# First tile ahead at the start of the second block's attention layers, and one weight chunk split by halves

## The chip, the cores and the metric

The kernel runs on one core of one Trainium2 chip. The metric is the device time of one execution in microseconds (us). PE is TensorE, DVE VectorE, ACT ScalarE, POOL GpSimd, SP the engine that issues most DMAs.

## The reference, cut to what matters

Two blocks of two transformer layers each, on 256 tokens of width 1024, all in float32. The second block is what the change touches, above all the two lines that begin a layer:

```
for l in range(2):
    proj = rms_norm(x, attn_norm[l]) @ w_in[l]        # [256, 1024] @ [1024, 2336]
    h_mla, h_diff, h_ch = split(proj, [416, 1568])
    o_mla  = rms_norm(mla_attention(h_mla, ...), mla_out_norm[l])
    o_diff = diff_attention(h_diff, ...)
    o_ch   = rms_norm(chunk_attention(h_ch, ...), chunk_out_norm[l])
    x = x + concat([o_mla, o_diff, o_ch]) @ w_out[l]
    x = x + conv_ffn(rms_norm(x, ffn_norm[l]), w_ffn_in[l], ..., w_ffn_out[l])
return rms_norm(x, final_norm)

def rms_norm(x, g):
    return x * rsqrt(mean(x * x, -1) + 1e-6) * g
```

## The kernel before

**Data and products.** The 256 tokens are two tiles of 128 rows, `X[:, t, :]` with `t` 0 or 1. Before a projection, the rows are scaled by the root of their mean square into `XH[:, t, :]`, transposed by PE in eight blocks of 128 features, and written as "features" `xh[:, k, tokens]` and `xl[:, k, tokens]`, `k` from 0 to 7. Each float32 factor is split in a high part (rounded, made by ACT: `xh`, `wh`) and a low part (the rest, made by DVE, for a few chunks by POOL: `xl`, `wl`), and one product is three matmuls, high x high, high x low, low x high (`mm3`). A matrix of weights comes in chunks of at most 1 MB: a DMA into one of four `raw` buffers, ACT's high part, DVE's low part, in two halves each. `J[name, i]` is a chunk's number, `weights(j)` splits a chunk on ACT and DVE, `weights_half(j, half)` half of it, `wait_chunk` makes PE wait for all of it. There are two places for split chunks, so that chunk n is split when PE has finished chunk n - 2 (`place_used`), and ACT and DVE run their own written order: each engine's program is a straight list of instructions, and they meet by semaphores.

**The start of a layer** (`l` 0 or 1; both look the same, with rows from a layer norm for l = 0, `own_rows`, and from an addition, `add_rows`, for l = 1). ACT squares each half row of both tiles (`square`), DVE adds the two sums (`mean_row`), POOL takes the power -1/2 (`rms`), DVE writes tile 0's scaled rows and the first half of tile 1's (`rms_rows`), ACT the second half of tile 1's (`rms_half`). PE first does `keep(0, 22)` or `keep(0, 6)`, matmuls of constants whose results are not used, then `rms_tiles`: for each k it transposes both tiles into one of four banks; ACT multiplies the 256 columns by the gain into `xh`, DVE makes `xl`. Then `part_tokens` multiplies chunks 0 and 1 of w_in (416 columns wide, four features each), for each feature both tiles:

```
            bs = {t: bank() for t in t2}
            part_tokens(0, 0, 416, bs, (win, 0))
            part_tokens(1, 1, 416, bs, (win, 0))
            for i in (2, 3, 4):
                for f in range(2):
                    column(i, f)
```

`column(i, f)` is 24 matmuls of 256 tokens by 128 columns of chunk i. Behind its features DVE has the distances between positions (`DIST`) and then chunk 2's low parts.

**The attention loop.** 11 units (six of two maps "diff", three "mla", two "chunk"). In turn i, PE does the transposes of unit i - 2, the scores of i, the values of i - 3, and some projection: in turn 4 and 5 `column(7, 0)` and `column(7, 1)` (chunk queries), in turn 6 and 7 chunk 8. DVE does in turn i `factors(i - 1)`, `turned`, the maxima of the scores of i, `normalise(i - 1)`, `mixed_low(i - 3)` (for odd diff units a reduction of squares that ACT makes after its exponentials of i), and then `beside(i)`, in which chunks are split: chunk 7 in turn 3, chunk 8 in turn 4, on ACT and DVE.

Of the kernel before, what the change touches and what calls it, by code (L numbers as in the profile page):

```python
# [144 lines left out]
def _build(nc, T, ctx):  # L145
# [3 lines left out]
    X = sb("X", [128, 4, 1024])  # L149
# [308 lines left out]
    def tensor_program(e, q):  # L458
# [486 lines left out]
        for l in range(2):  # L945
            A = ATT2[l]
            key, win = A.key, f"win{l}"
            span[:] = [0, 6]
            keep(0, (22, 6)[l])
            rms_tiles(("a", l), ("x1", 1) if l == 0 else ("f", 0))  # L950
            nb[0] = 5
            side = (S.ea, S.ev)
            side = (S.ea, S.ev)

            def part_tokens(i, part, w, bs, key):

                j = J[win, i]
                hv, lv = (v.rearrange("p (k n) -> p k n", k=4) for v in (hi_of(j), lo_of(j)))
                wait_chunk(j)
                for t in t2 if part == 0 else ():  # L960
                    wait_bank(bs[t])
                for k in range(4):
                    x = 4 * part + k
                    wait_feature(("a", l), x)
                    for t in t2:
                        tk = slice(128 * t, 128 * t + 128)
                        m = mm3(ps[bs[t]][:, 0:w], (xh[:, x, tk], xl[:, x, tk]), (hv[:, k, :], lv[:, k, :]), x == 0, x == 7)
                        if k == 3:
                            m.then_inc(*S.proj.up((key, t), ("use", j)))
                for t in t2 if part == 1 else ():  # L970
                    BANK[key, t] = bs[t]
                    free[bs[t]] = [(side[t], (key, t))]

            def column(i, f):

                j, b = J[win, i], bank()
                hv, lv = (v.rearrange("p (k n) -> p k n", k=8) for v in (hi_of(j), lo_of(j)))
                fs = slice(128 * f, 128 * f + 128)
                wait_chunk(j)
                wait_bank(b)  # L980
                for k in range(8):
                    m = mm3(ps[b][:, 0:256], (hv[:, k, fs], lv[:, k, fs]), (xh[:, k, 0:256], xl[:, k, 0:256]), k == 0, k == 7)
                m.then_inc(*S.proj.up(((win, i), f), ("use", j)))
                BANK[(win, i), f] = b
                free[b] = [(side[f], ((win, i), f))]
# [186 lines left out]

            bs = {t: bank() for t in t2}
            part_tokens(0, 0, 416, bs, (win, 0))
            part_tokens(1, 1, 416, bs, (win, 0))
            for i in (2, 3, 4):
# [111 lines left out]

    def feature_cols(key):
        g = key[2] if key[0] == "f" else key[1] if key[0] == "f1" else 0  # L1290
        return slice(256 * g, 256 * g + 256)

    def feature_slot(k):
# [7 lines left out]
    def feature_scales(key, k):  # L1301

        if key[0] in ("f", "f1"):
            g = key[-1]
            return sc[:, 0, k, g:g + 1], sc[:, 1, k, g:g + 1]
        kind, l = key
# [6 lines left out]
    def scalar_program(e, q):  # L1313
# [25 lines left out]
        def features(key, ks=range(8), wait=()):  # L1339

            for k in ks:
                q.wait_ge(*S.tr.at((key, k)))
                src, dst = ps[BANK.get((key, k), 0)][:, 0:256], xh[:, k, feature_cols(key)]
                s, s2 = feature_scales(key, k)
# [277 lines left out]
        block1_ffn(1, 1)  # L1622
        for t in t2:
            for half in range(2):
                square(("x1", 1), t, half, (S.vec, ("row", t, half)))
        rms_half(("x1", 1))


        for l in range(2):
# [12 lines left out]

            features(("a", l), wait=[(S.proj, ("use", used))])
            weights(after(J[win, 0]))
# [59 lines left out]
            def beside(i):  # L1704
# [8 lines left out]
                elif i == 10:  # L1713
                    turned_high(i)
                if i in (1, 2, 3, 4, 6, 8, 10):
                    weights(after({1: J[win, 5], 2: J[win, 6], 3: J[f"uq{l}", 0], 4: J[f"ukv{l}", 0], 6: J[win, 7],
                                   8: J[win, 8], 10: J[win, 9]}[i]))
# [29 lines left out]
            for t in t2:  # L1747
                for half in range(2):
                    square(("f", l), t, half, (S.vec, ("taken", f"fout{l}", t, half)))
            if l == 0:  # L1750
                rms_half(("f", l))

    def vector_program(e, q):
# [48 lines left out]
        def low(key, k):  # L1804
# [3 lines left out]
            if feature_kind(key) == "each":  # L1808
                r = e.scalar_tensor_tensor(dst, ps[BANK.get((key, k), 0)][:, 0:256], feature_scales(key, k)[0], high,
                                           ALU.mult, ALU.subtract)  # L1810
            else:
                r = e.tensor_tensor(dst, feature_slot(k), high, ALU.subtract)
# [490 lines left out]
        def own_rows(t, sides=(0, 1)):  # L2303
# [22 lines left out]
        own_rows(1, (1,))  # L2326
        rms_rows(("x1", 1), 0)
        mean_row(("x1", 1), 1)
        rms_rows(("x1", 1), 1, 512)


        for l in range(2):
# [17 lines left out]

            features(("a", l))
            for t, ks in enumerate(A.tiles):
# [141 lines left out]
            def beside(i):  # L2494
# [70 lines left out]
            if l == 0:  # L2565
                rms_rows(("f", l), 0)
                mean_row(("f", l), 1)
                rms_rows(("f", l), 1, 512)

# [15 lines left out]
    def gpsimd_program(e, q):  # L2585
# [145 lines left out]
    def sync_program(e, q):  # L2731
# [5 lines left out]
        for j, (name, i, w, kind) in enumerate(ORDER):  # L2737
# [24 lines left out]
            elif (name, i) in (("win0", 3), ("win1", 3)):  # L2762
                l = int(name[3])
                q.wait_ge(*S.tr.at((("a", l), 7)))
                e.dma_start(CB[:, :, :], T["rel"][l]).then_inc(*S.rel.up(l, by=16))
# [145 lines left out]
```

## Time and profile before

| | us |
|---|---|
| time, median of 3 runs | 1646.96 |
| lowest, highest | 1645.0, 1647.8 |
| the profiled execution, its time | 1644.66 |
| the profiled execution, span from first to last instruction | 1643.0 |
| PE busy in the span | 1597.2 (97%) |
| DVE, ACT, POOL busy | 1048.6 (64%), 804.0 (49%), 235.4 (14%) |

PE's busy time counts a matmul from its start to its modelled end, and matmuls overlap; keep matmuls count as busy too. Lines of the kernel in the profile (L486) are those of the program printed above; a helper's line serves all its callers: L486 to L488 are the three matmuls of `mm3`, L479 is `keep`, L528 the transposes of features, L1348 and L1809 their high and low parts, L1330 and L1775 the high and low parts of weights, L1443 `square`, L1449 `rms_half`, L2018 `rms_rows`, L2596 POOL's power.

### The profile page before, as it was taken

How to read it: one execution, taken by the hardware profiler on the slowest of the kernel's cores; microseconds unless marked ns; L12 is line 12 of the kernel's file. 1: busy time of each engine (PE TensorE's matmuls, PEld its weight loads, DVE VectorE, ACT ScalarE, POOL GpSimd, SP SyncE). 2: the span in 40 equal slices, each digit the busy share in tenths (PEclk: the TensorE clock that was granted, in tenths of full speed). 3: DMA queues.
4: the chain of work that ended last, by engine and by line, in shares of the span. 5: the costliest groups of instructions: out<-in, count | busy, mean ns of one | idle time of the engine just before them, and what ended most of it. 6: DMA issues, size and time to landing. Idle time of an engine off the chain costs nothing.

```text
span 1643.0 us, 26992 instructions
## 1 busy us (share of the span) xinstructions
PE 1597.2 (97%) x10894; PEld 1379.3 (84%) x10894; DVE 1048.6 (64%) x1938; ACT 804.0 (49%) x1517; POOL 235.4 (14%) x282
## 2 busy tenths in 40 slices
PE   7999999999999999999999999999999999999998
PEld 4788778887777888887899988878999888789986
DVE  3735856465354425787787767766776667767765
ACT  2414963332233423567455553655555556555553
POOL 0202410010110000012011101132111013311110
PEclk9999999999999999999999999999999999999999
DMA  9765122454564234021455552424555533335552
GB/s 368 291 243 200 37 81 84 157 202 154 214 253 174 77 103 154 10 76 45 180 180 206 180 195 106 149 83 154 180 180 184 191 136 125 129 135 189 186 197 77
DMA packets 39851, 257.28 MB, mean 157 GB/s; under 512 B 5552, under 2 KB 6832, under 8 KB 11056
## 3 DMA queue, kind: packets, MB, share of 16 engines
q1 hardware_dynamic: 36848, 249.61, 41.9%
q0 software_dynamic: 1296, 4.72, 0.9%
q8 instruction: 87, 1.43, 0.3%
q10 hardware_dynamic: 1584, 1.23, 0.2%
q14 instruction: 36, 0.29, 0.1%
HBM read 254.49 MB, written 1.05 MB: 156 GB/s over the span
## 4 chain that ended last, share of the span: by engine, by line
PE 83%; DVE 9%; ACT 4%; issue 2%; DMA 1%; ACTq 0%; POOL 0%; DVEq 0%; SPq 0%
PE ps L486 25%; PE ps L488 24%; PE ps L487 24%; PE ps L502 3%; PE ps L633 1%; PE ps L655 1%; PE ps L642 1%; DVE ps L2034 1%; DVE wl L1775 1%; PE ps L528 1%; PE ps L1081 1%; ACT arena L1681 1%; ACT wh L1330 1%; PE ps L614 1%; ACT arena L1401 1%
## 5 line engine op out<-in xcount | busy, mean ns | idle before, releaser
L1775 DVE TENSOR_TENSOR wl<-raw,wh 128x1024 fp32r<-128x1024 f32 (+2 forms) x322 | 375.9, 1209 | 349.8 <-ACT wh L1330 349.2
L1330 ACT CAST wh<-raw 128x1024 fp32r<-128x1024 f32 (+1 forms) x332 | 326.7, 1034 | 490.0 <-PE ps L488 400.3
L486 PE MATMUL ps<-xh,wh 128*128 128x256 f32 (+1 forms) x1582 | 493.5, 312 | 2.7 <-issue 2.4
L488 PE MATMUL ps<-xh,wl 128*128 128x256 f32 (+1 forms) x1582 | 488.6, 309 | 0.0
L487 PE MATMUL ps<-xl,wh 128*128 128x256 f32 (+1 forms) x1582 | 488.5, 309 | 0.0
L486 PEld LDWEIGHTS ps<-xh,wh 128*128 128x128 f32 x1582 | 301.8, 191 | 28.0 <-issue 12.0
L488 PEld LDWEIGHTS ps<-xh,wl 128*128 128x128 f32 x1582 | 301.8, 191 | 15.3
L487 PEld LDWEIGHTS ps<-xl,wh 128*128 128x128 f32 x1582 | 301.9, 191 | 15.1 <-issue 0.7
L486 PE MATMUL ps<-wh,xh 128*128 128x512 f32 (+3 forms) x812 | 297.7, 367 | 1.0 <-issue 0.8
L488 PE MATMUL ps<-wh,xl 128*128 128x512 f32 (+3 forms) x812 | 293.2, 361 | 0.0
L487 PE MATMUL ps<-wl,xh 128*128 128x512 f32 (+3 forms) x812 | 293.1, 361 | 0.0
L2119 DVE SCALAR_TENSOR_TENSOR arena<-ps,pv,arena 128x254 f32<-128x254 f32 (+2 forms) x352 | 192.6, 547 | 16.2 <-ACT arena L1495 6.9
L486 PEld LDWEIGHTS ps<-wh,xh 128*128 128x128 f32 x812 | 153.1, 189 | 30.0 <-issue 7.5
L488 PEld LDWEIGHTS ps<-wh,xl 128*128 128x128 f32 x812 | 153.1, 189 | 22.7
L487 PEld LDWEIGHTS ps<-wl,xh 128*128 128x128 f32 x812 | 153.3, 189 | 21.8 <-issue 0.5
L2636 POOL TENSOR_TENSOR arena<-arena 128x256 f32<-128x256 f32 (+1 forms) x88 | 81.9, 931 | 608.1 <-ACT arena L1480 608.1
L2596 POOL TENSOR_TENSOR st<-st,cs 128x1 f32<-128x1 f32 (+2 forms) x46 | 37.6, 818 | 510.4 <-DVE st L1951 236.3
L1495 ACT ACTIVATE arena<-ps,pv 128x256 f32<-128x256 f32 (+1 forms) x176 | 98.8, 609 | 13.7 <-PE ps L488 13.7
L502 PE MATMUL ps<-raw,silp 128*32 128x256 f32 x768 | 49.6, 393 | 9.2 <-DVE silp L2143 7.5
L1401 ACT ACTIVATE arena<-ps,st 128x512 f32<-128x512 f32 (+1 forms) x80 | 49.9, 644 | 8.8 <-DVE st L2034 5.0
L2626 POOL TENSOR_SCALAR arena<-arena,st 128x512 f32<-128x512 f32 (+1 forms) x40 | 34.4, 865 | 137.5 <-DVE st L2064 137.5
L1681 ACT ACTIVATE arena<-ps,st 128x128 f32<-128x128 f32 x88 | 35.9, 420 | 37.1 <-DVE st L2410 19.3
(214 smaller groups left out, 1835.8 us busy)
## 6 DMA issues: line engine op xcount, KB each, us to landing
raw<-in_ada SPq DMA_DIRECT2D x48, 1024.0 KB, 6.2
raw<-in_up SPq DMA_DIRECT2D x44, 1024.0 KB, 5.0
raw<-in_fin SPq DMA_DIRECT2D x44, 1024.0 KB, 4.8
raw<-in_down SPq DMA_DIRECT2D x22, 1024.0 KB, 4.8
raw<-in_fout SPq DMA_DIRECT2D x22, 1024.0 KB, 4.8
raw<-in_win SPq DMA_DIRECT2D x12, 1024.0 KB, 4.9
raw<-in_ev_w_in SPq DMA_DIRECT2D x9, 1024.0 KB, 7.1
raw<-in_wout SPq DMA_DIRECT2D x8, 1024.0 KB, 4.9
```

The lines of the kernel that those rows point to most:

```text
L486: e.matmul(out, A[0], B[0], start=first, stop=False)
L487: e.matmul(out, A[0], B[1], start=False, stop=False)
L488: return e.matmul(out, A[1], B[0], start=False, stop=last)
L502: m = e.matmul(ps[b][32 * g:32 * g + 32, 0:256], silp[:, k, 14 - 2 * i:46 - 2 * i], wv[:, k, :], start=(i == 0 and k < 4), stop=(last and ...
L1330: e.copy(hi_of(j)[:, a:b], raw_of(j)[:, a:b]).then_inc(*S.hi.up((j, half)))
L1401: e.activation(A.P[A.slot(i)][:, m, ks], A.scores(i)[:, m, ks], ACT.Exp, bias=mx[:, n:n + 1], scale=-1.0 if key == "od" or u["h"] >= 8 els ...
L1495: e.activation(temp(up, f)[:, part, 0:n], ps[2 * (f % 3) + part][:, 0:n], ACT.Identity, bias=w[3], scale=w[1 if up[0] == "u" else 2]).then ...
L1681: e.activation(A.P(i)[:, m, ks], ps[m][:, ks], ACT.Exp, bias=mx[:, c:c + 1], scale=1.0 if A.kind(i) == "mla" else -1.0, accum_out=sm[:, c: ...
L1775: e.tensor_tensor(lo_of(j)[:, a:b], raw_of(j)[:, a:b], hi_of(j)[:, a:b].bitcast(F), ALU.subtract).then_inc(*S.lo.up((j, half)))
L2119: e.scalar_tensor_tensor(acc[:, :, lo:hi], src[:, :, lo + shift:hi + shift], conv(row, f + NT * part), acc[:, :, lo:hi], ALU.mult, ALU.add ...
L2596: e.tensor_tensor(out, in_, minus_half[:, 0:n], ALU.pow).then_inc(*S.gps.up(key))
L2636: e.tensor_tensor(ACTF[:, f, 0:n], t[:, 1, 0:n], t[:, 0, 0:n], ALU.mult).then_inc(*S.prod.up((up, f)))
```

## The change

On all engines the first tile's features and products are put ahead of the second tile's. Features now have keys `("a", l, t)` and are 128 columns wide. ACT scales tile 0's rows (`rms_first`), DVE the first half of tile 1's, ACT its second half. PE's keep is 16 and 3 instead of 22 and 6. PE's products of chunks 0 and 1 are `first_rows(t, xs, bs)`, three matmuls for each tile and feature. `column` waits for its chunk by halves. The splits of chunk 7 move: on ACT half 0 ahead of turn 3's exponentials and half 1 behind them; on DVE half 0 in turn 3 and half 1 in turn 4; chunk 8's low parts on DVE from turn 4 to turn 5.

```
-            keep(0, (22, 6)[l])
-            rms_tiles(("a", l), ("x1", 1) if l == 0 else ("f", 0))
+            keep(0, (16, 3)[l])
...
+            made = ("x1", 1) if l == 0 else ("f", 0)
+            def first_features(t, ks):
+                features(("a", l, t), (t,), ks, [6, 7, 2, 3, 4, 5] if t else [4, 5, 6, 7, 2, 3],
+                         lambda k: [(S.act if t == 0 or k >= 4 else S.vec, ("xr", *made, t, k // 4))])
+            def first_rows(t, xs, bs):
+                tk = slice(128 * t, 128 * t + 128)
+                for x in xs:
+                    j = J[win, x // 4]
+                    hv, lv = (v.rearrange("p (k n) -> p k n", k=4) for v in (hi_of(j), lo_of(j)))
+                    if x % 4 == 0:
+                        wait_chunk(j)
+                    if x == 0:
+                        wait_bank(bs[t])
+                    wait_feature(("a", l, t), x)
+                    m = mm3(ps[bs[t]][:, 0:416], (xh[:, x, tk], xl[:, x, tk]), (hv[:, x % 4, :], lv[:, x % 4, :]), x == 0, x == 7)
...
# column(i, f), PE
-                wait_chunk(j)
                 wait_bank(b)
                 for k in range(8):
+                    q.wait_ge(*S.hi.at((j, k // 4)))
+                    q.wait_ge(*low_done(j, k // 4))
...
             bs = {t: bank() for t in t2}
-            part_tokens(0, 0, 416, bs, (win, 0))
-            part_tokens(1, 1, 416, bs, (win, 0))
+            first_features(0, range(6))
+            first_rows(0, [0], bs)
+            first_features(0, [6])
+            first_rows(0, [1], bs)
+            first_features(0, [7])
+            first_rows(0, [2, 3, 4], bs)
+            for x in range(5, 8):
+                first_features(1, [2 * x - 10, 2 * x - 9])
+                first_rows(0, [x], bs)
+            for x in range(2):
+                first_rows(1, [x], bs)
+                first_features(1, [6 + x])
+            first_rows(1, range(2, 8), bs)
...
# ACT
+        def rms_first(key):
+            q.wait_ge(*S.gps.at(("rs", key, 0)))
+            for half in range(2):
+                hs = slice(512 * half, 512 * half + 512)
+                e.mul(XH[:, 0, hs], X[:, 0, hs], cols((key, 0, "r"), 1)).then_inc(*S.act.up(("xr", *key, 0, half)))
+        def first_tile(l, key, last, used):
+            wait = [(S.proj, ("use", used))]
+            features(("a", l, 0), [0], wait)
+            square(key, 1, 1, last)
+            features(("a", l, 0), range(1, 4), wait)
+            rms_half(key)
+            features(("a", l, 0), range(4, 8), wait)
...
# ACT, ahead of layer 0 (ahead of layer 1 the same with ("f", 0))
-        for t in t2:
-            for half in range(2):
-                square(("x1", 1), t, half, (S.vec, ("row", t, half)))
-        rms_half(("x1", 1))
+        for half in range(2):
+            square(("x1", 1), 0, half, (S.vec, ("row", 0, half)))
+        rms_first(("x1", 1))
+        square(("x1", 1), 1, 0, (S.vec, ("row", 1, 0)))
...
-            features(("a", l), wait=[(S.proj, ("use", used))])
+            first_tile(l, ("x1", 1) if l == 0 else ("f", 0),
+                       (S.vec, ("row", 1, 1) if l == 0 else ("taken", "fout0", 1, 1)), used)
+            features(("a", l, 1))
             weights(after(J[win, 0]))
...
# ACT, the loop; beside(3) had weights(chunk 7)
+                if i == 3:
+                    weights_half(J[win, 7], 1)
...
             for i in range(A.n + A.lag + 1):
                 if 0 <= i - A.lag < A.n:
                     turned(i - A.lag)
+                if i == 3:
+                    weights_half(J[win, 7], 0)
                 if i < A.n:
                     softmax(i)
...
# DVE
+        def first_tile(l, key):
+            low(("a", l, 0), 0)
+            mean_row(key, 1)
+            low(("a", l, 0), 1)
+            low(("a", l, 0), 2)
+            rms_rows(key, 1, 512)
+            for k in range(3, 8):
+                low(("a", l, 0), k)
...
-        rms_rows(("x1", 1), 0)
-        mean_row(("x1", 1), 1)
-        rms_rows(("x1", 1), 1, 512)
+        first_tile(0, ("x1", 1))
...
-            features(("a", l))
+            features(("a", l, 1))
...
# DVE, beside(i)
                 elif i == 3:
                     copy2(("kn", l, 1), KN[:, 1, :])
+                    weights_half(J[win, 7], 0)
                 elif i == 4:
+                    weights_half(J[win, 7], 1)
                     copy2(("vm", l, 1), VM[:, 1, :])
...
-                if i in (1, 2, 3, 4, 11):
-                    weights(after({1: J[win, 5], 2: J[win, 6], 3: J[f"uq{l}", 0], 4: J[f"ukv{l}", 0], 11: J[win, 9]}[i]))
+                if i in (1, 2, 5, 11):
+                    weights(after({1: J[win, 5], 2: J[win, 6], 5: J[f"ukv{l}", 0], 11: J[win, 9]}[i]))
...
# POOL (rotation product) and SP (table of chunk attention, ahead of chunks 4 and later)
-            q.wait_ge(*S.tr.at((("a", l), 7)))
+            q.wait_ge(*S.tr.at((("a", l, 1), 7)))
```

## Rows read from the trace of the kernel before

**Rows 1.** The page's chain that ended last, by engine, share of the span
```profile
PE 83%; DVE 9%; ACT 4%; issue 2%; DMA 1%; ACTq 0%; POOL 0%; DVEq 0%; SPq 0%
```
**Rows 2.** Timeline of PE, start of layer 0: start, length, what, idle before
```profile
989.29 9.66 PE L479 MATMUL ps<-cs 128*128 128x256 f32 x44
1000.77 1.06 PE L528 MATMUL ps<-cs,arena 128*128 128x128 f32 x8 [1.83 <-DVE arena L2018]
1002.36 1.94 PE L528 MATMUL ps<-cs,arena 128*128 128x128 f32 x8 [0.52 <-DVE xl L1809]
1003.95 0.70 PE L486 MATMUL ps<-home,xh 128*128 128x416 f32 x1
...
1005.14 0.47 PE L486 MATMUL ps<-home,xh 128*128 128x416 f32 x1
...
1013.72 0.28 PE L486 MATMUL ps<-xh,wh 128*128 128x256 f32 x1
```
**Rows 3.** Timeline of PE, start of layer 1, and transposes before its feed-forward part
```profile
1316.58 2.75 PE L479 MATMUL ps<-cs 128*128 128x256 f32 x12
1319.78 1.06 PE L528 MATMUL ps<-cs,arena 128*128 128x128 f32 x8 [0.45 <-DVE arena L2018]
...
1322.67 0.42 PE L486 MATMUL ps<-home,xh 128*128 128x416 f32 x1
...
1331.79 0.28 PE L486 MATMUL ps<-xh,wh 128*128 128x256 f32 x1
...
1446.70 1.06 PE L528 MATMUL ps<-cs,arena 128*128 128x128 f32 x8 [2.14 <-DVE arena L2018]
```
**Rows 4.** Windows of 1 us: busy time by engine, granted PE clock third from last
```profile
1002.00:1003.00 1.00, 0.64 (x3) 0.63 (x4) 1.00 (x4) 0.79 (x3) 0.00 (x0) 0.50 0.00 0
...
1005.00:1006.00 1.00, 1.00 (x5) 0.97 (x5) 0.97 (x4) 1.00 (x2) 0.08 (x1) 0.81 0.26 49
...
1446.00:1447.00 1.00, 0.30 (x3) 0.33 (x4) 0.49 (x1) 0.72 (x1) 0.03 (x1) 1.00 0.12 49
```
**Rows 5.** Timelines of POOL, ACT and DVE, start of layer 0; last, a narrow ACT operation
```profile
994.89 1.06 POOL L2596 TENSOR_TENSOR st<-st,cs 128x1 f32<-128x1 f32 x2 [6.68 <-DVE st L1951]
998.49 0.63 ACT L1443 ACTIVATE arena<-X 128x512 f32<-128x512 f32 x1 [0.73 <-DVE X L2315]
...
1000.14 0.72 ACT L1449 ACTIVATE arena<-X,st 128x512 f32<-128x512 f32 x1 [0.93 <-POOL st L2596]
1001.22 1.57 ACT L1348 ACTIVATE xh<-ps,pv 128x256 fp32r<-128x256 f32 x4 [0.36 <-PE ps L528]
...
1000.14 0.48 DVE L2018 TENSOR_SCALAR arena<-X,st 128x512 f32<-128x512 f32 x1 [0.66 <-POOL st L2596]
1001.73 1.66 DVE L1809 SCALAR_TENSOR_TENSOR xl<-ps,pv,xh 128x256 fp32r<-128x256 f32 x4 [1.10 <-ACT xh L1348]
...
1036.01 0.37 ACT L1681 ACTIVATE arena<-ps,st 128x128 f32<-128x128 f32 x1 [0.51 <-DVE st L2410]
```
**Rows 6.** Timelines of POOL and ACT, start of layer 1
```profile
1314.89 0.54 POOL L2596 TENSOR_TENSOR st<-st,cs 128x1 f32<-128x1 f32 x1 [51.19 <-DVE st L2012]
...
1317.50 0.63 ACT L1443 ACTIVATE arena<-X 128x512 f32<-128x512 f32 x1 [2.00 <-DVE X L2559]
```
**Rows 7.** Timeline of DVE, low parts of chunks 2 and 3, layer 0
```profile
1006.56 2.28 DVE L1775 TENSOR_TENSOR wl<-raw,wh 128x1024 fp32r<-128x1024 f32 x2
...
1016.37 3.21 DVE L1775 TENSOR_TENSOR wl<-raw,wh 128x1024 fp32r<-128x1024 f32 x2 [0.39 <-ACT wh L1330]
```
**Rows 8.** Timelines of ACT, DVE and PE around chunk 7, layer 0
```profile
1052.04 0.37 ACT L1681 ACTIVATE arena<-ps,st 128x128 f32<-128x128 f32 x1 [1.53 <-DVE st L2410]
...
1055.27 2.36 DVE L1775 TENSOR_TENSOR wl<-raw,wh 128x1024 fp32r<-128x1024 f32 x2 [1.63 <-ACT wh L1330]
...
1057.73 0.36 PE L486 MATMUL ps<-xh,wh 128*128 128x256 f32 x1 [1.05 <-issue]
...
1066.64 0.55 PE L1092 MATMUL ps<-cs,arena 128*128 128x128 f32 x3 [0.89 <-DVE arena L2433]
```

More of the change, by code:

```diff
@@ L948, in tensor_program @@
             span[:] = [0, 6]
-            keep(0, (22, 6)[l])
-            rms_tiles(("a", l), ("x1", 1) if l == 0 else ("f", 0))
+            keep(0, (16, 3)[l])
             nb[0] = 5
             side = (S.ea, S.ev)
-            side = (S.ea, S.ev)
+            made = ("x1", 1) if l == 0 else ("f", 0)
[13 more added lines that the diff above has]
+                    m = mm3(ps[bs[t]][:, 0:416], (xh[:, x, tk], xl[:, x, tk]), (hv[:, x % 4, :], lv[:, x % 4, :]), x == 0, x == 7)
+                    if x == 7:
+                        m.then_inc(*S.proj.up(((win, 0), t), *([("use", j)] if t else [])))
+                    elif x == 3 and t:
+                        m.then_inc(*S.proj.up(("use", j)))
+                BANK[(win, 0), t] = bs[t]
+                free[bs[t]] = [(side[t], ((win, 0), t))]
             def part_tokens(i, part, w, bs, key):
@@ L963, in part_tokens @@
                     x = 4 * part + k
-                    wait_feature(("a", l), x)
                     for t in t2:
@@ L1289, in feature_cols, with feature_width @@
     def feature_cols(key):
+        if key[0] == "a":
+            return slice(128 * key[2], 128 * key[2] + 128)
         g = key[2] if key[0] == "f" else key[1] if key[0] == "f1" else 0
         return slice(256 * g, 256 * g + 256)
+    def feature_width(key):
+        return 128 if key[0] == "a" else 256
     def feature_slot(k):
@@ L1305, in feature_scales @@
             return sc[:, 0, k, g:g + 1], sc[:, 1, k, g:g + 1]
-        kind, l = key
+        kind, l = key[:2]
         if kind == "m":
@@ L1342, in features @@
                 q.wait_ge(*S.tr.at((key, k)))
-                src, dst = ps[BANK.get((key, k), 0)][:, 0:256], xh[:, k, feature_cols(key)]
+                src, dst = ps[BANK.get((key, k), 0)][:, 0:feature_width(key)], xh[:, k, feature_cols(key)]
                 s, s2 = feature_scales(key, k)
@@ L1714, in beside @@
                     turned_high(i)
-                if i in (1, 2, 3, 4, 6, 8, 10):
-                    weights(after({1: J[win, 5], 2: J[win, 6], 3: J[f"uq{l}", 0], 4: J[f"ukv{l}", 0], 6: J[win, 7],
+                if i == 3:
+                    weights_half(J[win, 7], 1)
+                if i in (1, 2, 4, 6, 8, 10):
+                    weights(after({1: J[win, 5], 2: J[win, 6], 4: J[f"ukv{l}", 0], 6: J[win, 7],
                                    8: J[win, 8], 10: J[win, 9]}[i]))
@@ L1748, in scalar_program @@
                 for half in range(2):
-                    square(("f", l), t, half, (S.vec, ("taken", f"fout{l}", t, half)))
+                    if l or not t or not half:
+                        square(("f", l), t, half, (S.vec, ("taken", f"fout{l}", t, half)))
             if l == 0:
-                rms_half(("f", l))
+                rms_first(("f", l))
     def vector_program(e, q):
@@ L1808, in low @@
             if feature_kind(key) == "each":
-                r = e.scalar_tensor_tensor(dst, ps[BANK.get((key, k), 0)][:, 0:256], feature_scales(key, k)[0], high,
+                r = e.scalar_tensor_tensor(dst, ps[BANK.get((key, k), 0)][:, 0:feature_width(key)], feature_scales(key, k)[0], high,
                                            ALU.mult, ALU.subtract)
@@ L2565, in vector_program @@
             if l == 0:
-                rms_rows(("f", l), 0)
-                mean_row(("f", l), 1)
-                rms_rows(("f", l), 1, 512)
+                first_tile(1, ("f", l))
         def final_rows(t, half):
@@ L2763, in sync_program @@
                 l = int(name[3])
-                q.wait_ge(*S.tr.at((("a", l), 7)))
+                q.wait_ge(*S.tr.at((("a", l, 1), 7)))
                 e.dma_start(CB[:, :, :], T["rel"][l]).then_inc(*S.rel.up(l, by=16))
```

## The prediction

> **What bounds the kernel now.** I read the page first, then the PE timeline at the two places that the change names, then what ACT, DVE and POOL do just ahead of them. The chain that ended last is PE for 83% [rows 1], so a microsecond counts only where PE stands still or does nothing useful. The start of each layer of the second block is such a place. In layer 0 the last product of the block before is issued by 989.29; then come 22 keep-warm matmuls (44 records, 9.66 us), an idle 1.83 us, eight transposes, an idle 0.52 us, eight more, and the first product at 1003.95. The first 416 columns take 16 product rows (8 features by 2 tiles) of three matmuls; they end where the next product starts, 1013.72 [rows 2]. In layer 1 the same: 1316.58, six keep matmuls, first transposes 1319.78, first product 1322.67, next stage 1331.79 [rows 3]. So a start costs 14.7 us in layer 0 and 6.1 us in layer 1, in which PE does no product. What holds the products back is in the ACT, DVE and POOL rows: the squares of the second tile's last half (ACT 998.49), its root on POOL, for which ACT stands idle 0.93 us, the scaled rows (1000.14, 0.72 us), then feature by feature ACT's high part and DVE's low part of both tiles together [rows 5]. The first tile was ready long before: its root is the second of the two POOL operations from 994.89, that is 995.95 [rows 5]. The kernel makes its first product wait for the second tile.
>
> **Part 1: the first tile by itself, layer 0.** Nothing is added to PE: 16 transposes and 48 matmuls remain, in another order; keep falls from 22 to 16 matmuls, at 9.66/22 = 0.44 us each, so it ends at 989.29 + 7.03 = 996.3. ACT takes the first tile's scaling from DVE: two halves of 512 at 0.72 us (about 0.64 apart): 995.98 to 997.3. Then the square of (tile 1, half 0) until 998.0, and the first feature. A feature is now 128 columns wide. Nothing in this stage shows that width; the nearest is an ACT operation of 128x128 from PSUM that lasts 0.37 us alone; the 256-wide ones come 1.57/4 = 0.39 (ACT) and 1.66/4 = 0.42 us (DVE) apart [rows 5]. I take 0.28 and 0.26 us per feature, a fixed part and a part that halves (bounds: half of the wide ones, 0.20, and all of it, 0.42). So 16 narrow features cost ACT 4.5 instead of 3.2 us, DVE 4.2 instead of 3.4.
> The path from there: high part of feature 0 done 998.35, low part 998.7, first product 998.85 (an estimate of 0.15 from DVE to PE: the idle 0.52 between the transposes less one feature's 0.39 [rows 2, 5]). ACT then turns to the square of (1,1) at 998.49 as before, so features 1 to 3 come at 999.2 to 1000.1, their low parts from 999.6; DVE's half of the second tile's rows lies between (1000.14 to 1000.6), ACT's too (until 1000.8). Product row 1 (three matmuls at (1013.72 - 1003.95)/48 = 0.20, 0.19 in layer 1, so 0.57) starts at 1000.05, and from there low parts arrive every 0.3 to 0.6 us, with feature 4's at about 1001.5: PE is the slower of the two. Left are 15 rows of 0.57 = 8.55 us and ten transposes of about 0.13 (1.06/8) = 1.3 us. The stage ends at 1000.05 + 9.85 = 1009.9 instead of 1013.72: 3.8 us gained, if PE runs at 2.4 GHz.
>
> **The clock.** In layer 0 the granted clock is 0.50 (1.2 GHz) at 1002 to 1003, after PE had stood idle 1.83 and 0.52 us with eight transposes between. At 1446.70 PE had stood idle 2.14 us and then did the same eight transposes [rows 3], and the clock stayed at 1.00 [rows 4]. So such a stretch may cost the clock or not. The loss now is the two starts' difference from first transposes to next stage: 12.95 against 12.01 us [rows 2, 3], 0.9 us. After the change PE is as thinly fed from 996.3 to 1000 (idle about 2.3 us of 3.7); if the clock falls, rows 1 to 4 run at the rate of the slow rows (three matmuls from 1003.95 to 1005.14, 0.40 us each at most against 0.19 [rows 2]; I take 0.35), costing about 1.5 us. Layer 0 is thus worth 3.8 (clock lost now, kept after), 2.9 (kept in both) or 2.3 (lost in both). Executions will differ; I take 2.9 for the median.
> The Trainium skill, "TensorE: Matmul & The Clock Gate", Part 4: PE-mode transpose, says that transposes do not count as PE being busy for the clock. By that rule the layer-0 fall is as it should be, but the stretch at 1446.70 speaks against it; it would bring the fall in layer 1 too, which is rival 1: by the rule the sum is 3.3 us, by the row 5.4.
>
> **Layer 1.** The first tile is ready while PE still multiplies: its root starts at 1314.89 [rows 6], ACT's two halves end at 1316.8. Keep is 3 matmuls, ending 1317.95. Feature 0's high part 1318.4 to 1318.8, first product 1319.25. ACT meets feature 0 before the square of (1,1), which slips from 1317.50 [rows 6] to 1318.7, and all behind it nearly by as much; row 1 of the products starts at 1320.3, and 9.85 us on is 1330.1 against 1331.79: 1.7 us. The keep matmuls cost 0.7 of it: with none the first product could start earlier.
>
> **What comes behind the start.** The second tile's transposes are spread between products, so its last features leave ACT at about 1006.9 instead of 1004.71, and only then does ACT split the next weights (win chunk 2), DVE after it: half 0's low part at about 1009.7, half 1's at 1010.9, where before both were done at 1008.84 (1006.56 + 2.28) [rows 7]. PE wants them at 1009.9 and, since a column now waits by half, 1011.4: nothing lost, 0.3 at most. Chunk 3: DVE ended it at 1019.58, just as PE needed it (1013.72 + 5.8), slowed by POOL to 3.21 us for what else takes 2.28 [rows 7]. After: ACT 1012.2 to 1014.2, DVE until 1016.3; PE needs half 0 at 1015.7 and half 1 at 1017.2. Covered with 0.9 to spare, and without the half-wait it would cost 0.6. The SP queue's table load stands behind the last transpose, 1004.30 before (1002.36 + 1.94 [rows 2]), at about 1006.3 now, with three chunks queued behind; the next is wanted at 1015.7, so this is hidden by 4 us. POOL's rotation product too.
>
> **Part 2: chunk 7 by halves.** PE waits 1.05 us at 1057.73 for chunk 7, whose low parts DVE makes 1055.27 to 1057.63 after waiting 1.63 for ACT, while ACT had stood idle 1.53 before the exponentials at 1052.04 [rows 8]. Half 0 on ACT moves into that idle time (free). DVE then does half 0 at 1053.6 to 1054.8 and goes on to the next unit's maxima, 2.7 us earlier than before. But half 1 stands on DVE behind a reduction that waits for ACT's square, which ACT makes after the four exponentials (1.6 us from their start); these start at 1055.9 now, so I get 1058.0 for the reduction and 1059.7 for half 1. So PE starts column 7 at once (1056.7), stops in its middle 1.6 us, and is 0.7 us late at the next unit. There it gets that back and more: the 0.89 us wait at 1066.64 for DVE [rows 8] is gone, because chunk 8's split, which stood before that unit's maxima, now stands behind them. Net 0.35 to 0.45 us a layer, 0.8 for both. Bounds per layer: -0.7 (nothing comes back) to +1.9 (both waits gone).
>
> **Sum.** 2.9 + 1.7 + 0.8 = 5.4 us. The profiled execution (1644.66, span 1643.0) lost the clock in layer 0; against it the sum is 3.8 + 1.7 + 0.8 = 6.3, or 1638.4. The median of the runs is 2.3 us above it, and nothing in the trace says that this difference goes: 1646.96 - 5.4 = 1641.5.
>
> **Rivals.**
> 1. Clock lost in both layers: layer 0 2.3, layer 1 1.7 - 1.5 = 0.2, with 0.8: 3.3 us, 1643.7. For it: in layer 1 PE has a thin stretch from 1317.95 to 1320.3. Against: it holds some 0.9 us of idle time only, less than the 2.14 that cost nothing. 0.10. By the rule named above, of the Trainium skill, this is the case that comes; by the row at 1446.70 it is not.
> 2. The gain is given back at chunk 3 (or 2): DVE now does 16 low parts and is itself late; if narrow features cost as much as wide ones (0.42), DVE is 2.6 us later in each start, PE is fed at 0.42 instead of 0.57 per row, still enough, but chunk 2 comes at 1012.3, whose second half PE wanted at 1011.4, and chunk 3 near 1018, wanted at 1017.2; with POOL's slowing (3.21 - 2.28 = 0.9) on top about 2 us are gone in each layer: 5.4 - 3.9 = 1.5 us, 1645.5. 0.12.
> 3. Slower: the clock, once down, stays at 1.2 GHz through the products, since these are now fed one row at a time. A matmul then costs 0.35 instead of 0.19. It decides from (5.4 + 3.3)/0.16 = 54 slow matmuls of the 96 in both layers; all 96 would cost 15 us: 1646.96 - 5.4 + 15 = 1656.6. Against: the clock is back within 1005 to 1006 after four matmuls in a row [rows 2, 4]. Chance of slower 0.06.
> 4. The change does not do what it says: if the first tile's products wait for something else of the second tile. The only such order is ACT's square (1,1) between features 0 and 1 (counted). 0.05 for 0 to 1 us: 1646.5.
> 5. More: both chunk-7 waits go and the clock holds: 3.8 + 1.7 + 2 x 1.5 = 8.5, 1638.5. 0.07.
>
> **Numbers.** Forecast 0.60. Its own range is 2.3 + 1.4 + 0 to 3.8 + 2.0 + 2 = 3.7 to 7.8 us: 1639.2 to 1643.3. The asked range adds rival 5 and most of 1 and 2: 1638.6 to 1645.3. 0.2% is 3.3 us, about what can be told from no change: faster below 1643.67. Forecast 0.58 of its 0.60, rival 5, half of rival 1 and 0.07 of the rest: 0.77. Same 0.17, slower 0.06.
>
> **What would show it.** The first 416-column product about 5 us earlier in layer 0 (near 999) and 3.4 in layer 1 (near 1319.2); the first 256-column product at about 1010 and 1330; ACT features of 128 columns 0.28 apart; no issue wait of PE at chunks 2 and 3; in column 7 a wait in its middle instead of before it, and none at the transposes after. Wrong if chunk 2 or 3 holds PE, if the clock row shows 0.50 in layer 1, or if the middle wait exceeds 2 us.

## The result, and the profile after

| | before | after |
|---|---|---|
| median of 4 runs, us | 1647.38 | 1636.49 |
| lowest, highest | 1645.0, 1648.02 | 1634.79, 1639.71 |
| profiled execution, its time | 1644.66 | 1636.88 |
| its span | 1643.0 | 1635.6 |

The ratio is 0.9939, with a 95% interval of [0.9927, 0.9952]: 10.0 us faster, between 7.9 and 12.0 (the medians of the table differ by 10.9). The forecast was 1641.5 us, with a range from 1638.6 to 1645.3. The sign was right; the gain was about twice the 5.4 us of the sum, and the measured 1636.49 lies below the range.

The page's chain that ended last, by engine, and its line on PE:

```profile
PE 85%; DVE 8%; ACT 4%; issue 1%; DMA 1%; ACTq 0%; POOL 0%; DVEq 0%; SPq 0%
...
PE 1593.0 (97%) x10876; PEld 1375.6 (84%) x10876; DVE 1047.8 (64%) x1952; ACT 809.3 (49%) x1537; POOL 238.2 (15%) x282
```

Timeline of PE after, start of layer 0, which answers to [rows 2]:

```profile
991.36 7.07 PE L479 MATMUL ps<-cs 128*128 128x256 f32 x32
998.84 1.05 PE L528 MATMUL ps<-cs,arena 128*128 128x128 f32 x6 [0.42 <-ACT arena L1495]
1000.95 0.43 PE L486 MATMUL ps<-home,xh 128*128 128x416 f32 x1 [1.05 <-DVE xl L1871]
...
1002.08 0.43 PE L486 MATMUL ps<-home,xh 128*128 128x416 f32 x1 [0.21 <-ACT xh L1387]
...
1011.73 0.36 PE L486 MATMUL ps<-xh,wh 128*128 128x256 f32 x1
```

Start of layer 1, and the transposes at the end of its attention part, for [rows 3]:

```profile
1313.75 1.46 PE L479 MATMUL ps<-cs 128*128 128x256 f32 x6
1315.04 0.82 PE L528 MATMUL ps<-cs,arena 128*128 128x128 f32 x6
1316.25 0.43 PE L486 MATMUL ps<-home,xh 128*128 128x416 f32 x1 [0.39 <-DVE xl L1871]
...
1326.76 0.35 PE L486 MATMUL ps<-xh,wh 128*128 128x256 f32 x1
...
1439.22 1.07 PE L528 MATMUL ps<-cs,arena 128*128 128x128 f32 x8 [0.53 <-DVE arena L2080]
```

From the first keep matmul, the first product of layer 0 comes after 9.59 us instead of 14.66, and chunk 2 begins after 20.37 instead of 24.43; in layer 1 it is 2.50 instead of 6.09 and 13.01 instead of 15.21. One more line has changed, in a place that the change does not name: the last one waited 2.14 us for DVE [rows 3] and now waits 0.53.

ACT and DVE after at the start of layer 0 show the new order and the narrow features, for [rows 5]:

```profile
998.06 1.34 ACT L1495 ACTIVATE arena<-X,st 128x512 f32<-128x512 f32 x2 [2.91 <-POOL st L2666]
999.31 0.61 ACT L1482 ACTIVATE arena<-X 128x512 f32<-128x512 f32 x1
...
999.92 0.35 ACT L1387 ACTIVATE xh<-ps,pv 128x128 fp32r<-128x128 f32 x1
...
1002.85 1.12 ACT L1387 ACTIVATE xh<-ps,pv 128x128 fp32r<-128x128 f32 x4
```

```profile
1003.23 1.13 DVE L1871 SCALAR_TENSOR_TENSOR xl<-ps,pv,xh 128x128 fp32r<-128x128 f32 x4 [0.27 <-ACT xh L1387]
```

Four narrow features take ACT 1.12 us and DVE 1.13, a quarter of which is 0.28 on both (forecast, in the same way of counting, 0.28 and 0.26). Their starts are 0.26 us apart, since one alone takes ACT 0.35.

**Stages of all profiles.** Spans of single executions say little here, because the part of the program before the change ends anywhere from 989.3 to 993.7 us; the first profile of before had the earliest end, so that the two spans of the table differ by 7.4 us only. So I cut every PE timeline at the same marks. "up" is where layer 0's keep begins; "start" runs from a layer's first keep matmul to the first 256-column product; "attention" from there to the next keep; "feed" from the transposes behind the attention part of layer 0 to layer 1's keep; "tr" is PE's idle time ahead of the transposes behind layer 1's attention part; "tail" from these transposes to the end of the span. All but "tr" are differences of starts in the timelines. The keep matmuls between an attention part and the transposes behind it, about 2.75 us each time, are in no column:

```
                    span   up     start0 att0   feed   start1 att1   tr   tail
before              1643.0 989.29 24.43 110.05 189.53 15.21 110.02 2.14 196.30
e4_before_again     1647.5 993.73 23.50 110.00 189.52 15.18 110.03 2.11 197.40
e6_keep26           1645.4 991.78 23.48 109.95 189.52 15.44 110.00 2.12 197.09
e5_before_dve4      1645.5 993.03 24.79 109.99 189.52 15.23 110.04 0.53 196.34
e3_pool_after_dve   1644.3 993.13 23.48 110.07 189.54 15.21 109.96 0.53 196.35
e2_chunk7_only      1642.1 990.48 23.50 109.08 189.53 15.19 109.06 2.14 197.09
e11_columns_halves  1645.2 991.95 23.47 109.70 189.53 15.21 109.68 2.12 197.52
e12_chunk8_later    1643.2 991.89 23.50 108.88 189.52 15.21 108.85 2.14 197.18
e1_start_only       1640.6 992.99 21.50 109.79 189.52 14.16 109.76 0.53 196.32
after               1635.6 991.36 20.37 109.21 189.53 13.01 109.18 0.53 196.38
e9_after_again      1636.1 991.95 20.38 109.19 189.53 13.02 109.18 0.53 196.29
e8_keep_16_1        1633.3 990.07 20.39 109.13 189.52 12.15 109.14 0.53 196.33
e7_half1_early      1633.3 991.37 21.84 107.36 189.52 13.03 107.33 0.53 196.29
e10_both            1630.4 990.86 20.36 107.29 189.53 12.16 107.30 0.53 196.34
```

The same stage of different executions agrees within 0.1 us, except where the clock fell (24.43, 24.79 and 21.84 in start0, and the tails of 197.1 and more) and in "up".

### The profile page after: what moved, and what is told of

Read it like the earlier page. It is cut to its first block, busy times and chain, and to the rows that moved or that the text cites. A ratio compares the mean times of both kernels' runs of the same rounds, so it can differ in the third digit from the quotient of the medians.

```text
span 1635.6 us, 27020 instructions
## 1 busy us (share of the span) xinstructions
PE 1593.0 (97%) x10876; PEld 1375.6 (84%) x10876; DVE 1047.8 (64%) x1952; ACT 809.3 (49%) x1537; POOL 238.2 (15%) x282
## 3 DMA queue, kind: packets, MB, share of 16 engines
HBM read 254.49 MB, written 1.05 MB: 156 GB/s over the span
## 4 chain that ended last, share of the span: by engine, by line
PE 85%; DVE 8%; ACT 4%; issue 1%; DMA 1%; ACTq 0%; POOL 0%; DVEq 0%; SPq 0%
PE ps L486 25%; PE ps L488 25%; PE ps L487 25%; PE ps L502 3%; PE ps L633 1%; PE ps L655 1%; PE ps L642 1%; DVE ps L2096 1%; PE ps L1104 1%; DVE wl L1843 1%; PE ps L528 1%; DMA raw<-in_ada 1%; PE ps L614 1%; ACT arena L1440 1%; ACT arena L1738 1%
## 5 line engine op out<-in xcount | busy, mean ns | idle before, releaser
L1837 DVE TENSOR_TENSOR wl<-raw,wh 128x1024 fp32r<-128x1024 f32 (+3 forms) x318 | 371.3, 1209 | 345.8 <-ACT wh L1369 345.2
L1369 ACT CAST wh<-raw 128x1024 fp32r<-128x1024 f32 (+2 forms) x328 | 322.6, 1033 | 489.0 <-PE ps L488 399.2
```

The source lines that it names most:

```text
L1369: e.copy(hi_of(j)[:, a:b], raw_of(j)[:, a:b]).then_inc(*S.hi.up((j, half)))
L1837: e.tensor_tensor(lo_of(j)[:, a:b], raw_of(j)[:, a:b], hi_of(j)[:, a:b].bitcast(F), ALU.subtract).then_inc(*S.lo.up((j, half)))
```

## The experiments

Each ratio is against runs of before made beside them: 1646.81 us (27 runs) for e1 to e4, 1646.53 (21) for e5 to e8, 1646.2 (21) for e9 to e12. Microseconds gained are worked out from the ratio. "By the stages" means from the table above, that is from one profiled execution each.

**The two parts alone.** e1_start_only is the changed kernel with chunk 7's splits, and the waits of `column`, as before:

```
# column(i, f), PE
+                wait_chunk(j)
                 for k in range(8):
-                    q.wait_ge(*S.hi.at((j, k // 4)))
-                    q.wait_ge(*low_done(j, k // 4))
# ACT, beside; the half splits around turn 3's exponentials go
-                if i in (1, 2, 4, 6, 8, 10):
+                if i in (1, 2, 3, 4, 6, 8, 10):
# DVE, beside; weights_half(J[win, 7], 0 and 1) go
-                if i in (1, 2, 5, 11):
+                if i in (1, 2, 3, 4, 11):
```

> The first tile ahead in both layers; chunk 7 and the waits of the columns as before. Theory A (the forecast's parts, with their sizes as the profile after shows them: start of layer 0 24.4 to 20.3 us, of layer 1 15.2 to 13.0): 6 to 6.5 us faster than before when both keep the clock and POOL's split of the last chunk does not meet DVE's; the late half of chunk 3 costs 0.3 to 0.6 us more per layer than in the changed kernel, so 5.5 us. Rival B (the surplus over the forecast comes from the starts alone, because the kernel before loses the clock there in most executions): 9 to 10 us faster. Rival C (the surplus comes with chunk 7's split): about 4 us.

e2_chunk7_only is the reverse, all of this put into the kernel before.

> Only chunk 7 by halves, chunk 8's low parts one turn later and columns that wait by halves; the start as before. Theory A: PE's 1.05 us wait ahead of column 7 becomes a wait of about 1.6 us in its middle, the 0.9 us wait after it goes: 0.45 us a layer there, and 0.2 a layer at chunk 3: 1.3 us faster in all. Rival B: the same or less. Rival C: 3 us or more faster, because the order of POOL and DVE at the end of the attention part changes.

Measured: e1 1640.86, ratio 0.9963 [0.995, 0.9975], 6.1 us faster (4.1 to 8.2); e2 1644.89, 0.999 [0.9981, 0.9999], 1.6 us (0.2 to 3.1). Together that is 7.7 us, a little less than the whole change's interval of 7.9 to 12.0, though their own intervals leave room for all of it. By the stages the parts do not simply add: the waits by half are worth something at chunk 2 only when the start is early. Rival B of e1 is out; rival C's 4 us is at the edge of the interval, but does not fit the stages, whose gains in e1 add up to 6.1. The attention parts gain 0.95 us a layer in e2 (110.03 to 109.07). Of these 0.3 are made at chunk 3, ahead of turn 4's transposes (39.64 us behind chunk 2's first product in before, 39.33 in e2), and 0.6 between these and turn 8's (25.48 and 24.87 us; 1053.36 and 1078.84 in before), where the columns of chunks 7 and 8 lie. In e1 the starts gain less than in the whole change, since PE now stands at chunk 2 in both layers:

```profile
1014.49 0.35 PE L486 MATMUL ps<-xh,wh 128*128 128x256 f32 x1 [1.05 <-DVE wl L1832]
...
1331.24 0.36 PE L486 MATMUL ps<-xh,wh 128*128 128x256 f32 x1 [1.05 <-DVE wl L1832]
```

The waits by half are thus worth 1.13 us in layer 0 (21.50 against 20.37) and 1.15 in layer 1, once the start is early. And the 2.14 us wait is already gone in e1.

**Before once more (e4).** The same program as before.

> The kernel before again, to see how its executions spread and where: within 0.2% of before. Theory A: its profile will differ from the first one by where the clock falls (start of layer 0, 650 to 700 us), by POOL and DVE meeting in layer 0, in layer 1 or in neither, and by 1 us or so of DMA waits in the first 60 us.

Measured: 1646.04, 1.0 [0.9992, 1.0009]. Its span of 1647.5 comes mostly from "up". The meeting of POOL and DVE, which was to be in layer 0, in layer 1 or in neither, came at the same place again. This execution kept the clock at the start of layer 0 (23.50) and lost it in layer 1's end, where the first profile had kept it. PE there, and windows of 1 us (granted clock third from last):

```profile
1450.10 1.06 PE L528 MATMUL ps<-cs,arena 128*128 128x128 f32 x8 [2.11 <-DVE arena L2018]
1451.68 1.94 PE L528 MATMUL ps<-cs,arena 128*128 128x128 f32 x8 [0.52 <-DVE xl L1809]
```

```profile
1451.00:1452.00 1.00, 0.48 (x4) 0.31 (x3) 0.95 (x3) 1.00 (x4) 0.00 (x0) 0.79 0.00 0
1452.00:1453.00 1.00, 1.00 (x7) 1.00 (x6) 0.82 (x3) 0.73 (x3) 0.00 (x0) 0.50 0.00 0
...
1455.00:1456.00 1.00, 1.00 (x10) 1.00 (x10) 0.90 (x1) 1.00 (x2) 0.00 (x0) 1.00 0.00 0
```

So my evidence that 2.14 us of idle time and eight transposes cost no clock was one lucky execution: the tail is 197.1 to 197.5 in five of the six profiles that have this wait, and 196.3 to 196.4 in the eight that do not have it. In all five, windows of 1 us there show a granted clock of 0.50, that is 1.2 GHz.

**Where the 2.14 us come from (e3, e5).** At the end of layer 1's attention part DVE and POOL make the low parts of two chunks, each from its own `raw` buffer into `home`, a place that keeps some split chunks. DVE in before, and DVE after at the same place:

```profile
1433.68 0.16 DVE L2488 TENSOR_SCALAR st<-ps 128x2 f32<-128x2 f32 x1 [1.40 <-PE ps L1142]
1434.13 4.57 DVE L1775 TENSOR_TENSOR home<-raw,home 128x1024 fp32r<-128x1024 f32 x2 [0.29 <-issue]
```

```profile
1427.81 0.16 DVE L2558 TENSOR_SCALAR st<-ps 128x2 f32<-128x2 f32 x1 [1.42 <-PE ps L1165]
1427.89 2.36 DVE L1837 TENSOR_TENSOR home<-raw,home 128x1024 fp32r<-128x1024 f32 x2
```

and POOL beside it, in before and after:

```profile
1433.92 0.70 POOL L2596 TENSOR_TENSOR st<-st,cs 128x2 f32<-128x2 f32 x1 [2.22 <-DVE st L2488]
1434.59 6.38 POOL L2591 TENSOR_TENSOR home<-raw,home 128x1024 fp32r<-128x1024 f32 x2
```

```profile
1428.05 1.63 POOL L2666 TENSOR_TENSOR st<-st,cs 128x2 f32<-128x2 f32 x1 [2.23 <-DVE st L2558]
1429.64 5.24 POOL L2661 TENSOR_TENSOR home<-raw,home 128x1024 fp32r<-128x1024 f32 x2
```

In before, DVE pauses 0.29 us for no wait that the profile shows. In that pause POOL begins its power, which takes 0.70 us, and its long split starts 0.46 us after DVE's: the two run side by side, DVE's takes 4.57 us instead of 2.36 and POOL's 6.38 instead of 5.24. Of the 2.2 us that DVE loses, 1.6 arrive at PE's transposes, which wait for rows that DVE makes later. In after there is no pause: DVE is first, POOL's power takes 1.63 us beside it, and POOL's split starts when DVE's is nearly done. Layer 0 of the kernel before, with the same code, was already like that:

```profile
1115.71 2.36 DVE L1775 TENSOR_TENSOR home<-raw,home 128x1024 fp32r<-128x1024 f32 x2
```

```profile
1115.87 1.63 POOL L2596 TENSOR_TENSOR st<-st,cs 128x2 f32<-128x2 f32 x1 [2.25 <-DVE st L2488]
```

e3 keeps the pause and takes the meeting away, in the kernel before:

```
# POOL, ahead of weights(after(J[f"wout{l}", 3]))
+            q.wait_ge(*S.lo.at((J[f"fin{l}", 0], 1)))
```

> The kernel before with one wait more: POOL starts its low parts of the last chunk of each attention part only when DVE has ended its own of the chunk before it. The profile before showed DVE at 4.57 us for two halves in layer 1 against 2.36 in layer 0, while POOL worked beside it, and PE idle 2.14 against 0.53 us. Theory A: this meeting is luck of an execution; taken away it saves 1.6 us per meeting, so 1 to 2 us of the median if it happens in most executions, else nothing. Rival: POOL is later by about 0.5 us and the rows behind it too: 0 to 0.5 us slower per layer.

e5 gives DVE a few more instructions early in the program, zeros written over zeros, and a wait:

```
# DVE, kernel before, behind e.memset(silp ...)
+        q.wait_ge(*S.vec.last())
+        for n_ in range(4):
+            e.memset(silp[:, 0:1, 2 * n_:2 * n_ + 2], 0.0).then_inc(*S.vec.up())
+        q.wait_ge(*S.vec.last())
```

> The kernel before with four tiny DVE memsets (of zeros that are zeros already) ahead of the first product, where DVE stands idle. In four executions with the old DVE program DVE paused 0.27 to 0.29 us ('issue') at one and the same instruction, the low part of the last chunk but one of layer 1's attention, and POOL slipped in ahead of it; in two executions with the new DVE program it did not. Theory A: the pause belongs to a place in DVE's stream of instructions. Shifted by five instructions it falls into a wait; DVE's two halves take 2.36 us, PE's idle before the transposes is 0.53 instead of 2.14, and the time falls by 1.6 us. Rival: it belongs to the moment (what POOL, PE and the DMAs do then): nothing changes, idle 2.1 us.

Measured: e3 1645.01, 0.9992 [0.9983, 1.0], 1.3 us, which by itself is at the edge of no change; e5 1644.93, 0.9987 [0.9978, 0.9995], 2.1 us (0.8 to 3.6). DVE in e3, then DVE and PE in e5:

```profile
1436.97 2.36 DVE L1775 TENSOR_TENSOR home<-raw,home 128x1024 fp32r<-128x1024 f32 x2 [0.27 <-issue]
```

```profile
1437.83 2.36 DVE L1775 TENSOR_TENSOR home<-raw,home 128x1024 fp32r<-128x1024 f32 x2
...
1449.16 1.07 PE L528 MATMUL ps<-cs,arena 128*128 128x128 f32 x8 [0.53 <-DVE arena L2018]
```

With the meeting gone, by either way, the wait is 0.53 us and the tail 196.3: 1.6 us of idle time and mostly 0.9 of clock, some 2.5 us, which the intervals of both runs allow (e3's goes up to 2.8). In e3 the pause is there and costs nothing, so the meeting was not luck of an execution, as e3's expectation had it, but comes with the pause. In e5 the pause is gone, with nothing changed at or near its place, and another has come where no other profile has one:

```profile
765.27 0.16 DVE L2062 TENSOR_TENSOR st<-st 128x2 f32<-128x2 f32 x1 [0.27 <-issue]
```

So it hangs on where an instruction stands in DVE's stream. All seven profiles with as many DVE instructions up to there as before (before, e2, e3, e4, e6, e11, e12) have the pause, and the six of them without e3's wait have the meeting; e5 and the six with the first tile ahead, whose stream is longer too, have neither.

**Chunk 7 taken apart (e11, e12, e7).** e11 has only the half waits of `column` in the kernel before, e12 only DVE's split of chunk 8 in turn 5 instead of 4, with chunk 7 whole:

```
# e12: DVE, beside, kernel before
-                if i in (1, 2, 3, 4, 11):
+                if i in (1, 2, 3, 5, 11):
```

> The kernel before with nothing changed but that a column waits for its chunk by halves. Theory A: without the earlier start this brings only the 0.25 us a layer that PE waited for chunk 3 (it stood 0.37 instead of 0.12 us ahead of column 3) and, at column 7, the 1.05 us wait less one half (1.1 us), the rest of which goes on into the next transposes' wait for DVE: 0.3 to 1.3 us a layer in all, up to 2.6. Rival: the 1.05 us before column 7 come back wholly in the 0.89 us wait after it, since DVE's order is as before: 0.25 a layer, 0.5 us.

> The kernel before with DVE's low parts of chunk 8 in turn 5 instead of turn 4, chunk 7 whole as before. Theory A (what the 0.89 us wait at the transposes comes from): that wait goes, 0.9 us a layer, as DVE makes turn 5's maxima ahead of chunk 8; the 1.05 us ahead of column 7 stay: 1 to 1.8 us faster in all. Rival (chunk 8 then comes too late for column 8): no gain or a new issue wait of PE near column 8.

Measured: e11 1645.98, 0.9998 [0.9989, 1.0007], not to be told from before; by the stages 0.35 us a layer, made at chunk 3, near the rival's 0.25. At chunk 7 it gains nothing (25.46 us from turn 4's transposes to turn 8's, 25.48 before): PE has the 1.05 us wait of [rows 8] no more, but waits more at the next two units, 0.34 where it had waited for nothing and 1.40 in place of 0.89:

```profile
1061.47 0.55 PE L1093 MATMUL ps<-cs,arena 128*128 128x128 f32 x3 [0.34 <-DVE arena L2434]
...
1068.02 0.55 PE L1093 MATMUL ps<-cs,arena 128*128 128x128 f32 x3 [1.40 <-DVE arena L2434]
```

e12: 1644.76, 0.9989 [0.998, 0.9998], 1.8 us (0.3 to 3.3); by the stages 1.15 us a layer, somewhat more than expected. The 0.89 us wait is gone, and the 1.06 us at chunk 7 have stayed. So moving chunk 8's split is what pays. From turn 4's transposes to turn 8's it brings 1.16 us alone (24.32) and 0.6 with chunk 7 by halves as in the change: the halves, as placed there, take back 0.55. In the changed kernel PE stops in the middle of column 7, and DVE says why, in its line ahead of the second half's split:

```profile
1057.49 0.36 PE L486 MATMUL ps<-xh,wh 128*128 128x256 f32 x1 [1.60 <-DVE wl L1843]
```

```profile
1055.60 0.42 DVE L2525 TENSOR_REDUCE st<-arena 128x4 f32<-128x256 f32 x1 [0.65 <-ACT arena L1754]
...
1056.13 1.22 DVE L1843 TENSOR_TENSOR wl<-raw,wh 128x1024 fp32r<-128x1024 f32 x1
```

The split is queued behind a reduction that waits for ACT's square. e7 puts it ahead, in the changed kernel:

```
# DVE, the loop
                     softmax(i)
+                if i == 4:
+                    weights_half(J[win, 7], 1)
...
# DVE, beside
                 elif i == 4:
-                    weights_half(J[win, 7], 1)
```

> The changed kernel with DVE's half 1 of chunk 7 right after the maxima of turn 4 instead of behind the reduction that waits for ACT's square. Theory A (PE's 1.60 us wait in the middle of column 7 is DVE waiting for ACT): the wait goes wholly, 1.6 us a layer, against what normalise, 1.2 us later, costs: at least 1.2 us a layer, 2.5 to 3.2 us faster than the changed kernel. Rival (it comes back as a wait of the next transposes for normalise): 0 to 1 us.

Measured: 1634.66, 0.9927 [0.9914, 0.9941], 12.0 us below before (9.7 to 14.2). The time alone does not tell it from the change, whose 10.0 go from 7.9 to 12.0; the stages do. The profiled execution lost 1.5 us of clock at the start of layer 0 (21.84), but the attention parts take 107.36 and 107.33 instead of 109.2: 1.85 us a layer, 3.7 in all, where 2.5 to 3.2 were expected. PE has no wait from the transposes at 1052.63 to those at 1075.69:

```profile
1052.63 0.55 PE L1115 MATMUL ps<-cs,arena 128*128 128x128 f32 x3 [0.62 <-DVE arena L2503]
...
1075.69 0.88 PE L1115 MATMUL ps<-cs,arena 128*128 128x128 f32 x6 [0.58 <-DVE arena L2505]
```

**Keep (e6, e8) and both gains (e10), the change again (e9).** e6 is the kernel before with `keep(0, (26, 8)[l])`, e8 the changed kernel with `keep(0, (16, 1)[l])`, e10 has the edits of e7 and e8 together.

> The kernel before with 26 and 8 keep matmuls instead of 22 and 6, which end when the transposes are due. Theory A (clock): the start of layer 0 is 23.5 us in every execution and never 24.4; the median falls by the share of executions that lose the clock there, at most 0.9 us, since three of four profiles already had 23.5. Rival: the keep matmuls end after the rows and delay the transposes: 0 to 0.9 us slower.

> The changed kernel with 1 instead of 3 keep matmuls in layer 1. Theory A (in layer 1 the start waits for PE's keep, since the first tile's rows are ready when PE ends): the first product comes 1.6 instead of 2.5 us after the end of the products before, the start 12.1 instead of 13.0 us: 0.9 us faster. Rival: the clock falls in layer 1: the start takes 13.5 us or more.

> The changed kernel with half 1 of chunk 7 right after the maxima of turn 4 and 1 keep matmul in layer 1. Theory A: the two add up, 2 x 1.85 + 0.86 = 4.6 us less than the changed kernel, 1632 us. Rival: the clock falls in layer 1, now that PE is idle longer: 1 to 1.5 us of it are lost.

> The changed kernel again. Theory A (structural parts: starts 3.1 and 2.2 us at equal clock, attention 0.83 a layer, POOL meeting DVE in layer 1 1.6 us): 8.6 us faster than before, ratio 0.9948, with starts of 20.4 and 13.0 us (21.8 in layer 0 where the clock falls). Rival (something more than these, as the first 10.9 us between medians suggest): 10 us or more.

Measured: e6 1647.07, 1.0005 [0.9996, 1.0014]: no gain, and layer 1's start is 0.23 us longer. Layer 0's start kept the clock in its one profile (23.48), as it did in five of seven without the longer keep, so that the clock theory of e6 is neither shown nor refuted. e8 1636.42, 0.9942 [0.993, 0.9955]: layer 1's start is 0.86 us shorter (12.15), with the clock kept; the median cannot show it beside e9's 1636.19, 0.994 [0.9927, 0.9952]. That is 9.9 us (7.9 to 12.0) for the change a second time: it repeats, and the time cannot decide between e9's 8.6 and its rival's 10; 8.6 left out the 0.9 us of clock in the tail. e10 1631.55, 0.9915 [0.9901, 0.9928]: 14.0 us below before and 4.6 below the median of e9, as expected; by the stages 3.8 from e7 and 0.86 from e8, with the clock kept in layer 1. It is the fastest kernel of the study.

## Why the forecast came out too small, point by point

| term | forecast | measured |
|---|---|---|
| start of layer 0, equal clock | 2.9 | 3.1 |
| start of layer 1 | 1.7 | 2.2 |
| attention parts (chunks 3, 7, 8), both layers | 0.8 | 1.7 |
| end of layer 1's attention part | none | about 2.5 |
| sum | 5.4 | 9.5 |

The column "measured" is read from the stages, that is from single executions. Its sum is within the 10.0 [7.9, 12.0] of the runs.

- **The starts were right.** The first product of layer 0 was forecast 9.56 us behind the first keep matmul and came at 9.59; chunk 2 at 20.6 and came at 20.37. In layer 1: 2.67 and 13.5 against 2.50 and 13.01.
- **The clock.** As forecast, it falls in some executions and costs 1.5 us in a start of the new kind (21.84 against 20.37) and 0.9 to 1.3 in one of the old kind: in one of six profiles and in two of eight. Layer 1's start never lost it, so rival 1 did not come. But the row with which I argued against the rule, the transposes behind [rows 3]'s 2.14 us, proves nothing: e4 and four others lost the clock there. The Trainium skill, "TensorE: Matmul & The Clock Gate", Part 4: PE-mode transpose, says that transposes do not count as PE being busy in the same way. That fits those five; it does not fit the first profile, nor the five old starts of layer 0 (of seven; e6's longer keep left no idle time) that kept the clock with 1.8 us idle and sixteen transposes, if it is read as a certainty.
- **Chunks 2 and 3.** "Nothing lost, 0.3 at most" at chunk 2 was right, but only because of the waits by half, which I priced only at chunk 3, at 0.6. Without them 1.05 us are lost at chunk 2 in each layer (e1). At chunk 3 PE had stood idle about 0.25 us in before (0.37 between two matmuls where 0.12 is usual); this is gone, 0.23 a layer.
- **Chunk 7.** The wait in mid-column was forecast 1.6 and is 1.60, and the 0.89 us wait has gone. The gain of both layers was forecast 0.8 and is 1.2; with chunk 3's 0.5 the attention parts give 1.7. All of it comes from chunk 8's split (e12); chunk 7's halves, as placed, cost.
- **The step that failed** is in the sum itself: it has no term for the end of layer 1's attention part, and so puts it at nothing without a reason. What was measured there is about 2.5 us. Part of this was in the 2.3 us between the profiled execution and the median, of which the forecast says that "nothing in the trace says that this difference goes": some 0.9 us of it can be the clock in the tail, which the first profile happened to keep and the other five with this wait lost; the rest is mostly the early end of "up" in that profile.

  I had the row: the same transposes waited 2.14 us in layer 1 and 0.53 in layer 0. I used it as evidence on the clock, and never asked why two layers of the same program differ by 1.6 us. The difference was a meeting of DVE and POOL that any change of DVE's instruction count may undo, and this change undid it. The range had rival 5 for a larger gain, but from other waits; even its end, 1638.5, was not low enough.

  The three terms that the sum does have were too small by 1.6 us together (7.0 against 5.4), over half of it in the attention parts; alone they would have given 1640.0, inside the range.

That the meeting goes is a side effect and no merit of the idea: four stores of zeros and a wait (e5) do it as well. Of the 9.5 us, 7.0 belong to the change.

What the pause of 0.27 to 0.29 us is stays open. It is shown that it sits at one instruction in all seven profiles with the old number of instructions ahead, that in e5, with five more ahead, it is gone from there and one stands elsewhere, and what it costs at its old place. Its cause was not tried.

## What to carry to other kernels

- When two layers of the same code differ in one wait (2.14 against 0.53 us), find out why before pricing anything near it: such a wait is a term of its own, and an unrelated edit can remove or create it.
- A split placed behind an instruction that waits for another engine inherits that wait. Read what the instruction ahead of it waits for, and put it in front: here this gave 1.85 us a layer, three times the 0.6 us that the change gave there.
- Cut the timeline at the same marks in several profiles before comparing spans. Here the part before the change varies by 4.4 us, and every other stage by about 0.1 unless the clock falls.

## What the runs showed of the hardware that I had not expected

- DVE pauses 0.27 to 0.29 us at a fixed instruction without a wait that the profile shows, in all seven profiles with the same number of DVE instructions ahead, and no longer with five more ahead (e5), where a pause of 0.27 us stands at another instruction.
- Two splits of 128x1024 from SBUF, on DVE and POOL side by side, slow both: DVE 4.57 instead of 2.36 us, POOL 6.38 instead of 5.24, or instead of the 4.78 of e3, where POOL starts only when DVE has ended. POOL's small power took 1.62 or 1.63 us in the seven profiles in which DVE's split had begun before it, and 0.70 in the seven in which it had not.
- The clock fell to 1.2 GHz in five of six executions around 2.1 us of idle time and sixteen transposes, in two of seven around 1.8 us and as many, and in none where the idle time ahead of them was 0.5 us.
